# Seven-product pairs of a fused two-block kernel: a combination of VectorE moved ahead of two low parts, and another order of work at the entries

## What is computed

```python
def swiglu_2(x, w1, w2):
    g, u = jnp.split(x @ w1, 2, axis=-1)
    return (jax.nn.silu(g) * u) @ w2
```

## Time and profile before

| | |
|---|---|
| median of 3 executions | 3269.78 us (3268.66 to 3271.48) |
| the profiled execution, its own time | 3270.13 us |
| span of the profile | 3268.2 us |
| granted TensorE clock, mean | 0.998 of full speed |
| PE, DVE, ACT, POOL busy | 98%, 55%, 45%, 51% of the span |
| DMA | 98 GB/s over the span |

### The profile page before, as it was taken

How to read it: one execution, slowest core, us unless ns; L and a number is a source line. 1 busy time by engine, 2 the same in 40 slices (tenths; PEclk the granted TensorE clock), 3 DMA queues, 4 the chain that set the end, 5 groups by cost and what they waited for, 6 DMA issues and landing times.

```text
span 3268.2 us, 56968 instructions
## 1 busy us (share of the span) xinstructions
PE 3214.0 (98%) x19910; PEld 2857.4 (87%) x19910; DVE 1802.7 (55%) x3043; ACT 1481.0 (45%) x2585; POOL 1652.9 (51%) x1218
## 2 busy tenths in 40 slices
PE   7999999999999999999999999999999999999998
PEld 5778898999899988888888998899888888889987
DVE  5864886773277616344148771677245352177724
ACT  5544555553355423266235552455332473245533
POOL 3343113665456644545445664476535454446654
PEclk9999999999999999999999999999999999999999
DMA  7341002223222322223222232222323232222332
GB/s 295 129 168 58 1 1 91 90 103 118 88 89 104 116 97 84 97 91 103 97 89 80 103 116 98 70 103 103 116 78 104 97 99 95 96 78 94 109 112 84
DMA packets 90051, 322.36 MB, mean 99 GB/s; under 512 B 9776, under 2 KB 12208, under 8 KB 89776
## 3 DMA queue, kind: packets, MB, share of 16 engines
q1 hardware_dynamic: 88576, 316.65, 28.4%
q10 hardware_dynamic: 1328, 3.67, 0.3%
HBM read 318.19 MB, written 2.10 MB: 98 GB/s over the span
## 4 chain that ended last, share of the span: by engine, by line
PE 86%; DVE 8%; ACT 2%; issue 2%; POOL 1%; DMA 0%; POOLq 0%; DVEq 0%; SPq 0%
PE ps L639 10%; PE ps L640 10%; PE ps L644 10%; PE ps L1275 9%; PE ps L1283 9%; PE ps L1277 9%; PE ps L1315 3%; PE ps L1313 3%; PE ps L1320 3%; PE ps L1337 2%; PE ps L1343 2%; PE ps L1339 2%; PE ps L1121 2%; PE ps L1208 2%; DVE ps L2624 1%
## 5 line engine op out<-in xcount | busy, mean ns | idle before, releaser
L529 POOL TENSOR_TENSOR w_lo<-raw,w_hi 128x512 fp32r<-128x512 f32 x726 | 999.3, 1400 | 1150.2 <-ACT w_hi L1486 1149.8
L1486 ACT ACTIVATE w_hi<-raw 128x1024 fp32r<-128x1024 f32 x363 | 383.6, 1058 | 915.7 <-PE ps L644 478.3
L639 PE MATMUL ps<-acts,w_hi 128*128 128x512 f32 x1336 | 520.0, 389 | 0.0
L640 PE MATMUL ps<-acts,w_hi 128*128 128x512 f32 x1336 | 519.9, 389 | 0.0
L588 POOL TENSOR_TENSOR w_lo<-raw,w_hi 128x512 fp32r<-128x512 f32 x270 | 376.1, 1407 | 153.3 <-ACT w_hi L1875 153.3
L1275 PE MATMUL ps<-acts,w_hi 128*128 128x256 f32 x1440 | 364.1, 285 | 9.2 <-DVE tmp L2679 5.7
L1277 PE MATMUL ps<-acts,w_hi 128*128 128x256 f32 x1440 | 360.9, 283 | 0.0
L644 PE MATMUL ps<-acts,w_lo 128*128 128x512 f32 x1336 | 330.0, 389 | 0.0
L644 PEld LDWEIGHTS ps<-acts,w_lo 128*128 128x128 f32 x1336 | 250.8, 188 | 52.0
L640 PEld LDWEIGHTS ps<-acts,w_hi 128*128 128x128 f32 x1336 | 250.9, 188 | 51.8
L639 PEld LDWEIGHTS ps<-acts,w_hi 128*128 128x128 f32 x1336 | 250.8, 188 | 51.8
(11 more groups left out here) (454 smaller groups left out, 7096.4 us busy)
## 6 DMA issues: line engine op xcount, KB each, us to landing
raw<-stream SPq DMA_DIRECT2D x543, 512.0 KB, 3.4
ada_behind<-ada SPq DMA_DIRECT2D x32, 512.0 KB, 3.5
ada_first<-ada SPq DMA_DIRECT2D x8, 1024.0 KB, 14.0
X<-x_in ACTq DMA_DIRECT2D x1, 2048.0 KB, 8.6
out<-X SPq DMA_DIRECT2D x16, 128.0 KB, 1.7
xin<-x_in ACTq DMA_DIRECT2D x2, 768.0 KB, 6.9
xin<-x_in SPq DMA_DIRECT2D x2, 768.0 KB, 9.2
rope_sb<-rope SPq DMA_DIRECT2D x1, 1280.0 KB, 9.0
```

What stands on the lines that cost most here:

```text
L529: last = nc.gpsimd.tensor_tensor(w_lo[:, slot, part, :], raw[:, slot % RAW, part, :], f32(w_hi[:, slot, part, :]), ALU.subtract)
L639: mm(o, w_hi[:, s, k, :], xh, start=start, stop=False, skip_group_check=True)
L640: mm(o, w_hi[:, s, k, :], xl, start=False, stop=False, skip_group_check=True)
L1486: A(w_hi[:, s, :, :], raw[:, s % RAW, :, :], ACT.Copy).then_inc(s_hi, 1)
```

## The change

In a fast unit, VectorE's third combination (L2679) runs right behind weight sum four, ahead of the low part of operand 1 and, as before, of the low part of operand 3.

At each of the five entries the order is another. On VectorE, plain unit 2 (product and low part) comes ahead of the low part of `form_two` and of the weight sums, and the low part of operand 6 comes between product and low part of plain unit 3. On ScalarE, the silu and the hidden high part of plain unit 2 come ahead of the high part of `form_two`; operands 0 to 3 follow it; the silu of plain unit 3 comes ahead of operands 4 and 5. `plain_unit` is cut into `plain_product` and `plain_low`. No instruction is added or removed, and no DMA is issued from another place.

```diff
@@ ScalarE: fast_units
+            def sum_high(form, banks, n):
+                act.wait_ge(s_sums, sums.up(n))
+                for part, total in zip(pieces, in_banks(banks)):
+                    last = A(form[:, part, 0, :], total, ACT.Copy)
+                last.then_inc(s_hi, 1)
+
             def fast_units(at):
                 for unit in range(0, FAST_FROM - 2, 2):
                     plain_pair(unit)
-                for form, banks, n in ((form_one, 4, 1), (form_three, 6, 1), (form_two, 4, 2)):
-                    act.wait_ge(s_sums, sums.up(n))
-                    for part, total in zip(pieces, in_banks(banks)):
-                        last = A(form[:, part, 0, :], total, ACT.Copy)
-                    last.then_inc(s_hi, 1)
-                for j in range(2):
-                    for half in range(2):
-                        act.wait_ge(s_done, used.up())
-                        for i in range(4 * j + 2 * half, min(4 * j + 2 * half + 2, PRODUCTS)):
-                            operand(at, 0, i)
-                        if half == 0:
-                            silu(j)
-                        else:
-                            if j:
-                                A(form_four[:, :, 0, :], fourth_sum[:, :, :], ACT.Copy).then_inc(s_cs, 1)
-                            hidden_high(FAST_FROM - 2 + j)
+                sum_high(form_one, 4, 1)
+                sum_high(form_three, 6, 1)
+                act.wait_ge(s_done, used.up())
+                silu(0)
+                act.wait_ge(s_done, used.up())
+                hidden_high(FAST_FROM - 2)
+                sum_high(form_two, 4, 2)
+                for i in range(4):
+                    operand(at, 0, i)
+                act.wait_ge(s_done, used.up())
+                silu(1)
+                for i in (4, 5):
+                    operand(at, 0, i)
+                act.wait_ge(s_done, used.up())
+                operand(at, 0, 6)
+                A(form_four[:, :, 0, :], fourth_sum[:, :, :], ACT.Copy).then_inc(s_cs, 1)
+                hidden_high(FAST_FROM - 1)
@@ VectorE: plain_unit is cut in two
-            def plain_unit(unit, j):
+            def plain_product(j):
...
+            def plain_low(unit):
                 dve.wait_ge(s_prod, 2 + prod.up())
                 dve.wait_ge(s_hh, hh.up())
...
+            def plain_unit(unit, j):
+                plain_product(j)
+                plain_low(unit)
@@ VectorE: fast_unit
                     if formed:
                         weight_sum(1 - j, 2)
-                        low_of(1, sum_two)
                     dve.wait_ge(s_done, products + 4)
                     dve.wait_ge(s_comb, added + 2)
                     TT(gate_two, fourth, third, ALU.add).then_inc(s_comb, 1)
                     if formed:
+                        low_of(1, sum_two)
                         low_of(3, sum_one)
@@ VectorE: fast_hidden, the entry
                 last.then_inc(s_sums, 1)
                 sums.up()
+                plain_unit(FAST_FROM - 2, 0)
                 bank_low(form_two, 4, hi.up())
                 dve.wait_ge(s_slo, ffn * 3 * (FAST_UNITS + 1) + 3)
                 for n in range(3):
                     weight_sum(0, n)
-                plain_unit(FAST_FROM - 2, 0)
                 low_of(1, sum_two)
                 low_of(3, sum_one)
-                plain_unit(FAST_FROM - 1, 1)
+                plain_product(1)
                 low_of(6, sum_four)
+                plain_low(FAST_FROM - 1)
```

## The result

| | before | changed |
|---|---|---|
| median of 6 executions each | 3268.97 us (3268.40 to 3271.48) | 3281.41 us (3281.11 to 3284.64) |
| the profiled execution, its own time | 3270.13 us | 3283.47 us |
| its span | 3268.2 us | 3281.5 us |
| granted TensorE clock, mean | 0.998 | 0.998 |

A forecast was written before the change was run, and what follows sets the result against it. PE, busy 98% of the span, was taken as the bound, with 15.4 us to win at most. Per entry 3.15 - 0.67 = 2.48 us lost, five times 12.4, less 0.8: +11.6, so 3281.4 us; range 3264 to 3287.

The forecast's parts named there:

- Part 1: Fast units: the third combination, moved behind weight sum four, ends before product 6 needs it; that wait of PE goes.
- Unit 0: First fast unit of an entry: 0.58 us won, though product 5 starts later, released by GpSimd's low part of operand 5.
- The two terms put in front: Entry: plain unit 2's product (0.69 us) and high part (0.64) come first; low part and weight sums about 1.23 later.
- Unit 1: Second fast unit of an entry: product 5 waits for the second combination; 0.67 us won up to unit 2.
- The round: Repeating path through ScalarE, GpSimd and VectorE, without PE: 10.27 us against PE's 10.06, losing 0.21 in units 2 to 16.
- The lead: Unit 2: GpSimd's low part of operand 0 comes 0.67 us ahead of VectorE's weight sum one and wins each turn.
- The sum: Whole kernel: 2.48 us lost per entry, five times 12.4; the eleventh wait gives back 0.8: +11.6 us.
- the eleventh wait: PE's extra wait for the third combination, in the third entry's unit 2; its removal wins some 0.8 us.
- The rival on the other side: VectorE gets its turn in unit 1 already: 8.0 us won, 3261.8; chance 0.12, shared with everything going well.
- The first rival: The slow round ends at once after unit 1: 3265.6 us; chance 0.17 for ending at once or on the way.
- slow round: Units where GpSimd takes its turn ahead of weight sum one: 10.46 us before, forecast 10.27 in the new order.
- What would show it: Signs for the profile after: no L2679 waits, some 80 for L2673, units of 10.27 us, weight sum one of 1.45.

The follow-up runs named there:

- first experiment: Kernel before with only the third combination moved, the entries as they were: 3281.29 us, ratio 1.0034.
- experiment 8: Changed kernel with GpSimd's low part of operand 0 waiting for weight sum one, plus form_four copied and its low parts taken earlier at the entries: 3263.34 us, ratio 0.9985.
- 9: Changed kernel with the second combination ahead of weight sum two: 3278.95 us, ratio 1.0030 against the kernel before.
- second experiment: Changed kernel with the third combination put back behind the low part of operand 1, the entries' new order kept: 3269.63 us, ratio 1.0003.
- sixth: Kernel before, with ScalarE making the high part of operand 0 ahead of its copy of the first product: 3299.75 us, ratio 1.0096.
- third experiment: Changed kernel plus one wait: GpSimd's low part of operand 0 waits for VectorE's weight sum one, not at the entry: 3262.42 us, ratio 0.9978.
- seventh experiment: Changed kernel, with ScalarE making the high part of operand 0 ahead of its copy of the first product: 3282.97 us, ratio 1.0044.

## Why the prediction was right

It forecast 3281.4 us and 3281.41 was measured; that close an agreement is luck, as the terms show.

- **Part 1.** The wait for the third combination went in all entries, as said. Measured alone it is the whole effect (first experiment).
- **Unit 0** was forecast at 12.12 - 0.58 = 11.54 us and took 11.56; product 5 was forecast 8.57 behind product 0 and came at 8.59, released by GpSimd, as said (the second combination would have held it as long; experiments 8 and 9 show each of the two alone). That the entry's new order makes it 0.2 later is shown by the second experiment, whose unit 0 is 12.33; that it goes through `form_four` is read from the timeline, where GpSimd's low parts of it begin 3.65 us behind product 0 before (592.63 - 588.98) and 3.85 after (594.13 - 590.28). In ScalarE's timeline the copy of the weights' high part moved by 1.2 us against product 0 of unit 0, and that of `form_four` by 0.22 (forecast 1.23 and 0.23). The two terms put in front, 0.69 and 0.64, add up to 1.33 and not to 1.23; what took the tenth off is not said.
- **Unit 1** was forecast at 10.83 us and took 10.92. The term "product 5 starts 0.06 behind the second combination" was too small: it ended at 609.24 + 0.41 = 609.65 and product 5 began at 609.79, 0.14 later. The prediction took the 0.14 us between 608.14 and 608.28 of before as 0.06 of semaphore and 0.08 of slack; there was no slack in it, that is the whole step. So 12.12 + 10.92 - 11.56 - 10.92 = 0.56 us were won up to unit 2 in the first entry, and not 0.67.
- **The round** was forecast at 10.27 and is 10.26. It is shorter than the old one, 10.45, and the rows agree with the reason given: ScalarE's silu follows the copy ahead of it by 611.78 - 611.31 = 0.47 us, where it was 0.67. The copy for operand 4 stands behind that silu, and GpSimd had stood idle for it (0.22 us in unit 1 of before); now its low part of operand 4 follows that of operand 2 at once (612.80, above). Both rounds could be seen: the new one in the changed kernel and in the first experiment, the old one in the sixth. GpSimd's row of before, ScalarE's of after:

```profile
611.48 2.56 POOL L588 TENSOR_TENSOR w_lo<-raw,w_hi 128x512 fp32r<-128x512 f32 x2 [0.22 <-ACT w_hi L1875]
```
```profile
611.31 0.59 ACT L1875 ACTIVATE w_hi<-ps 128x512 fp32r<-128x512 f32 x1
611.78 0.42 ACT L1885 ACTIVATE tmp<-tmp 128x256 f32<-128x256 f32 x1
```
- **The lead** of GpSimd was forecast at 0.67 and is 0.61. Counted from the start of the second combination the weight sum came at 617.41 - 609.24 = 8.17, as forecast, and GpSimd at 7.56 instead of 7.50; most of that is the same 0.08 of slack that was none. That it is the lead which decides, and not something else of the new order, is shown from both sides: the order of the two forced, the round is 10.05 (third); the lead made larger in the kernel before, the round is slow there too (sixth).
- **The sum.** From product 0 of unit 0 to product 6 of unit 17 the five entries of before take 913.16 us and those of after 925.22: 12.06 lost, against 11.6 forecast. By terms: units 2 to 16 lose 3.15 to 3.17 us per entry (3.15), the entries win 2.93 in all (3.35), the eleventh wait gives 0.78 (0.8). The spans differ by 13.3. The other 1.3 us lie ahead of the first entry, where the two executions differ already (product 0 at 588.98 and at 590.28). Other profiles had it between 588.50 and 591.77, those with the entries of before (588.50 to 589.81) and those with the new ones (588.53 to 591.77) alike, so one execution can't say whether the change has a part in this. The medians differ by 12.4.
- **The rival on the other side** was priced at 3261.8 for VectorE winning in unit 1 already. The third experiment forces just that, and measures 3262.42. The first rival, 3265.6, would need a slow round that ends; it ended in no entry of the changed kernel.

One step under "What would show it" failed: "some 80 waits for L2673 at product 5". There are 5. Stalls of a tenth do not appear there; the product pitch had to be read from the timeline. Whoever had looked at the waits alone would have called the forecast wrong.

What stays open: whether the changed order would keep the fast pace once VectorE had won a turn, without a wait to force it. In the seventh experiment two entries did not keep it, but its exchange on ScalarE takes away just the order that puts VectorE ahead in the kernel before (645.25 to 646.23 above), so it does not decide this. A kernel of the changed order with a single forced turn was not tried.

## What to carry to other kernels

If two engines block each other inside instructions, look at the time between their issues in each unit, ahead of the shares: a tie of hundredths can be tipped by an instruction moved elsewhere, and a change that takes a wait off TensorE can lose more by turning it than the wait cost. Where it matters who goes first, say so with a semaphore on the engine that has slack; here one such wait was worth 0.58% of the changed kernel. And when a unit repeats dozens of times, measure the pitch of its units, since here a loss of 0.2 us in each appeared in no row of PE's waits.

## What the runs showed of the hardware

- VectorE's weight sum (two inputs in SBUF) takes 0.68 us alone and 1.45, in a tie 1.82, where GpSimd, also with two inputs in SBUF, had the turn ahead of it; it then ends 0.55 to 0.56 us behind GpSimd's end. GpSimd's 1.29 us becomes 1.35 to 1.85, so as to end 1.14 to 1.16 us behind VectorE's. The same numbers stand in before, after and the experiments. The Trainium skill ("SBUF — State Buffer", section "SBUF: two separate sides") has VectorE and GpSimd lock a shared pair exclusively, and the runs agree: in the pairs of weight sum one and low part of operand 0, over all fast units of before and of the changed kernel, the one that was issued first by 0.15 us or more had its turn first. At 0.01 to 0.03 us the start does not tell which one has it. So semaphores are not the only place where these two engines meet.
- An instruction that waits gets its turn at the end of the other engine's running one, also ahead of the next one that follows there without a pause. In experiment 8 VectorE's L2625, issued at 592.94 in the first of GpSimd's two, ends at 594.54, and GpSimd's second ends at 592.70 + 2.98 = 595.68, 1.14 behind it. In the same way GpSimd, issued at 616.80 during L2709, is next at 617.15, before the weight sum is issued at 617.41. That is what makes the slow round repeat.
- The step from the end of a VectorE addition to the matmul that it releases is not one number: 0.05 or 0.06 us at product 6 and at product 4 (unit 0 of before and after), 0.13 us at product 5 in all 75 units 2 to 16 after. In the kernel, PE has one more wait at product 5 behind that for the combination, the one for GpSimd's low part. Where that last wait ends last, in unit 0, the step from GpSimd's end is 0.06 again (598.81 to 598.87). This fits a wait more that costs 0.07 or 0.08 us; no run tests it.
